# A trunk layer's mixer: sixth gate unit, first branch, softmaxes and convolution taps in another order on three engines

## The reference, cut to what matters

```python
o, s_f, s_b = _gla_bidir(qa, ka, va, glog[:, :, 0], glog[:, :, 1], s0[:, 0], s0[:, 1])
o = o * lax.rsqrt(jnp.mean(jnp.square(o), -1, keepdims=True) + LN_EPS) * lp['gla_norm']
y_a = (o.reshape(b_, l_, GLA_V_W) * jax.nn.silu(ra)) @ lp['w_br_gla']
...
y_b = att @ lp['w_br_na']        # neighbourhood attention; a softmax per head
y_c = _conv_module(cvi, lp)      # depthwise convolution of 31 taps, LayerNorm, silu, projection
g = jax.nn.sigmoid(mg.reshape(b_, l_, 3, D_MODEL))
m = g[:, :, 0] * y_a + g[:, :, 1] * y_b + g[:, :, 2] * y_c
return m @ lp['w_out'], kb, vb, jnp.stack([s_f, s_b], 1)
```

## Time and profile before

| | |
|---|---|
| median of 3 runs | 2106.37 us |
| the profiled execution | 2109.81 us, span 2107.6 us |
| PE busy | 1909.7 us (91% of the span) |
| DVE busy | 1461.7 us (69%) |
| ACT busy | 1135.2 us (54%) |
| mean granted TensorE clock | 0.954 of full |
| chain that ended last | PE 87%, DVE 6%, ACT 3%, issue 2%, DMA 1% |

### The profile page before, as it was taken

One profiled execution on the slowest core, in us unless ns is written; L12 is line 12 of the kernel. 1 busy time (PEld: TensorE's weight loads), 2 busy tenths in 40 slices (PEclk: granted clock), 3 DMA queues, 4 the chain that ended last, 5 costly groups with the idle time before them and its releaser, 6 DMA issues.

```text
span 2107.6 us, 25160 instructions
## 1 busy us (share of the span) xinstructions
PE 1909.7 (91%) x9102; PEld 1429.3 (68%) x9102; DVE 1461.7 (69%) x1795; ACT 1135.2 (54%) x1352; POOL 29.8 (1%) x53
## 2 busy tenths in 40 slices
PE   4999959869996999959789999999999999999994
PEld 1875435447884874434368888888888888888883
DVE  1446474344455445682489898998989899898995
ACT  2442220234442542221168777877878788787882
POOL 1000010000000000010000000000000000000000
PEclk8999979979998999979889999999999999999997
DMA  9565422445656455413269999999999999999990
GB/s 347 182 226 206 172 85 80 160 159 191 214 198 244 165 184 192 148 46 120 92 247 370 347 355 343 352 361 341 362 350 351 368 332 362 345 359 345 354 363 34
DMA packets 226992, 529.61 MB, mean 251 GB/s; under 512 B 4824, under 2 KB 7328, under 8 KB 226928
## 3 DMA queue, kind: packets, MB, share of 16 engines
q1 hardware_dynamic: 222848, 516.96, 68.0%
q0 software_dynamic: 3168, 9.80, 1.5%
q10 hardware_dynamic: 912, 1.97, 0.3%
HBM read 526.10 MB, written 2.62 MB: 251 GB/s over the span
## 4 chain that ended last, share of the span: by engine, by line
PE 87%; DVE 6%; ACT 3%; issue 2%; DMA 1%; ACTq 0%; DVEq 0%; POOL 0%; SPq 0%; POOLq 0%
PE ps L805 19%; PE ps L807 19%; PE ps L806 19%; PE ps L738 15%; PE ps L759 2%; PE ps L762 2%; PE ps L761 2%; PE ps L772 2%; PE ps L1139 2%; PE ps L795 1%; DVE arena L1821 1%; PE ps L1160 1%; DMA ring<-in_w_mod 1%; PE ps L1038 1%; ACT arena L1252 1%
## 5 line engine op out<-in xcount | busy, mean ns | idle before, releaser
L2092 DVE TENSOR_TENSOR arena_r<-ring,arena_r 128x1024 fp32r<-128x1024 f32 x448 | 540.0, 1223 | 38.3 <-ACT arena_r L1544 16.9
L1544 ACT ACTIVATE arena_r<-ring 128x1024 fp32r<-128x1024 f32 x448 | 474.1, 1061 | 119.0 <-PE ps L807 117.9
L805 PE MATMUL ps<-arena_r 128*128 128x512 f32 x1128 | 447.4, 397 | 22.2 <-DVE arena_r L1596 13.9
L806 PE MATMUL ps<-arena_r 128*128 128x512 f32 x1128 | 440.9, 391 | 0.0
L807 PE MATMUL ps<-arena_r 128*128 128x512 f32 x1128 | 411.8, 391 | 0.0
L2092 DVE TENSOR_TENSOR ring_r<-ring,ring_r 128x1024 fp32r<-128x1024 f32 x224 | 271.0, 1223 | 41.0 <-ACT ring_r L1544 38.0
L1544 ACT ACTIVATE ring_r<-ring 128x1024 fp32r<-128x1024 f32 x224 | 235.7, 1060 | 61.3 <-PE ps L807 60.3
L805 PEld LDWEIGHTS ps<-arena_r 128*128 128x128 f32 x1128 | 213.7, 189 | 67.7 <-issue 23.2
L805 PE MATMUL ps<-ring_r,arena_r 128*128 128x512 f32 (+1 forms) x592 | 239.3, 404 | 17.1 <-DVE ring_r L1596 8.3
L807 PEld LDWEIGHTS ps<-arena_r 128*128 128x128 f32 x1128 | 213.6, 189 | 46.5
L806 PEld LDWEIGHTS ps<-arena_r 128*128 128x128 f32 x1128 | 213.9, 190 | 43.9
(11 more groups left out here) (243 smaller groups left out, 1952.0 us busy)
## 6 DMA issues: line engine op xcount, KB each, us to landing
ring<-in_moe_w_gate SPq DMA_DIRECT2D x56, 2048.0 KB, 7.8
ring<-in_moe_w_up SPq DMA_DIRECT2D x56, 2048.0 KB, 8.0
ring<-in_moe_w_down SPq DMA_DIRECT2D x56, 2048.0 KB, 8.3
ring<-in_w_in SPq DMA_DIRECT2D x28, 2048.0 KB, 10.1
ring<-in_w_mod SPq DMA_DIRECT2D x24, 2048.0 KB, 8.6
ring<-in_ffd_w_gate SPq DMA_DIRECT2D x5, 2048.0 KB, 9.5
ring<-in_ffd_w_up SPq DMA_DIRECT2D x5, 2048.0 KB, 7.8
ring<-in_ffd_w_down SPq DMA_DIRECT2D x5, 2048.0 KB, 7.7
```

Source lines behind the costliest of these rows:

```text
L805: mm(o_, hi, w_hi[:, n], start=start, stop=False)
L806: mm(o_, hi, w_lo[:, n], start=False, stop=False)
L1544: act_(split_part(j)[0], raw_part(j), ACT.Copy).then_inc(part_hi, 1)
L2092: V.tensor_tensor(w_lo, raw_part(j), w_hi.bitcast(F32), ALU.subtract).then_inc(part_lo, 1)
```

## The change

Only the order of existing work changes; no arithmetic is added or left out. On PE, `gla_states(1)`, `kbtok`, the scores of group 0 and `gla_out(1)` now stand ahead of `mgate(5)`; `gla_turn(1)`, `kctxT` and the bias stand behind it; `cvtok` and `PT` of group 0 come next, then `branch(0)`; `cvT` and the scores of group 1 come behind `branch(0)`, then `branch(2)`; `gate_rows(0)` stands ahead of `branch(1)`. On DVE, ten taps stand between carry and norm of group 0, six inside `gla_prepare(1)` ahead of its wait for the exponentials, three behind it; `softmax(0)` follows `gla_norm(1)` at once; `diagonal` and `softmax(1)` stand between `gated(0)` and `gated(2)`. ACT follows: the first softmax's exponential stands ahead of the sixth gate unit. `plan()` lists products in the new order, so banks are handed out by it; the order of weight units stays.

```diff
@@ tensor @@
                 gla_scores(1)
-                mgate(5)
                 gla_states(1)
-                gla_out(1)
-                gla_turn(1)
                 turned(("kbtok", l), [kbT[:, j * T:j * T + P] for j in range(4)])
...
                     full(ins, "sc", l, 0, i)
+                gla_out(1)
+                mgate(5)
+                gla_turn(1)
+                pe.wait_ge(ctx_in, 16 * (l + 1))
+                turned(("kctxT", l), [kctx[:, j * P:(j + 1) * P] for j in range(4)])
...
+                copied("oT", l, 0), copied("oT", l, 1)
+                branch(0, lambda g, k: o[:, g * 512 + k * P:g * 512 + (k + 1) * P])
+                for g in range(G):
+                    copied("cvtok", l, g)
+                    turned(("cvT", l, g), [acc[:, g * 512 + j * P:g * 512 + (j + 1) * P] for j in range(4)])
                 copied("kctxT", l)
...
                 gate_rows(0, diag1)
+                copied("attT", l, 0), copied("attT", l, 1)
+                branch(1, lambda g, k: attT[:, g * 512 + k * P:g * 512 + (k + 1) * P])
                 mod_unit(l, 10, mrow)
@@ scalar @@
                 gla_keys(1)
+                take(kbtok, ("kbtok", l))
+                gla_sqrt()
+                softmax_exp(1024)
+                mgate(5)
+                gla_turned(1)
+                take(kctxT, ("kctxT", l))
+                for i in range(2):
+                    take(PT[:, i * 512:(i + 1) * 512], ("PT", l, 0, i))
+                norm_sqrt(2)
@@ vector @@
                     st.done(V.tensor_scalar(karg, karg, EXP_CAP, None, ALU.min), args_ready)
+                    if g:
+                        conv_taps(22, 28)
                     st.next(exps_ready)
...
                 gla_carry(0)
+                conv_taps(12, 22)
                 gla_norm(0)
                 gla_prepare(1)
-                conv_taps(12, 22)
+                conv_taps(28, TAPS)
                 gla_mask(1)
                 gla_carry(1)
                 gla_norm(1)
-                conv_taps(22, TAPS)
+                softmax(0)
                 mod_columns(4, 10, 32)
...
                 conv_norm()
-                softmax(0)
-                softmax(1)
...
                 gated(0)
+                diagonal(diag1, 16, 0)
+                softmax(1)
                 gated(2)
-                diagonal(diag1, 16, 0)
                 gated(1)
```

More of the change, by code:

```diff
@@ L167, in plan, with branch @@
         p("keT", l, 1), p("att", l, 1, 0), p("att", l, 1, 1)
+        p("kv", l, 1, 0), p("kv", l, 1, 1)
+        p("kbtok", l), p("sc", l, 0, 0), p("sc", l, 0, 1)
+        p("o", l, 1)
         mg(l, 5)
[L169 to L172, removed]
+        p("oT", l, 1)
+        p("kctxT", l), p("bias", l, 0), p("bias", l, 1)
         p("cvtok", l, 0), p("cvtok", l, 1)
-        p("cvT", l, 0), p("cvT", l, 1)
         p("PT", l, 0, 0), p("PT", l, 0, 1)
-        for i in range(4):
-            p("sc", l, 1, i)
-        for b in (0, 2):
+        def branch(b):
             for g in range(G):
@@ L181, in plan @@
             u(("br", l, b), ("y", l, b, 1, 1))
+        branch(0)
+        p("cvT", l, 0), p("cvT", l, 1)
+        for i in range(4):
+            p("sc", l, 1, i)
+        branch(2)
         p("attT", l, 0)
@@ L186, in plan @@
         for g in range(G):
-            p("y", l, 1, g, 0), p("y", l, 1, g, 1)
-        u(("br", l, 1), ("y", l, 1, 1, 1))
-        for g in range(G):
             p("gbc", l, 0, g, 0), p("gbc", l, 0, g, 1)
+        branch(1)
         mod(l, 10)
@@ L957, in _ @@
                 gla_scores(1)
-                mgate(5)
                 gla_states(1)
-                gla_out(1)
-                gla_turn(1)
                 turned(("kbtok", l), [kbT[:, j * T:j * T + P] for j in range(4)])
-                pe.wait_ge(ctx_in, 16 * (l + 1))
-                turned(("kctxT", l), [kctx[:, j * P:(j + 1) * P] for j in range(4)])
-                pe.wait_ge(bias_in, 64 * (l + 1))
-                for i in range(2):
-                    full(mm(claim("bias", l, i), C("flip"), bias[:, i * 512:(i + 1) * 512], start=True, stop=True),
-                         "bias", l, i)
                 for i in range(2):
@@ L976, in _ @@
                     full(ins, "sc", l, 0, i)
+                gla_out(1)
[3 more added lines that the diff above has]
+                turned(("kctxT", l), [kctx[:, j * P:(j + 1) * P] for j in range(4)])
+                pe.wait_ge(bias_in, 64 * (l + 1))
+                for i in range(2):
+                    full(mm(claim("bias", l, i), C("flip"), bias[:, i * 512:(i + 1) * 512], start=True, stop=True),
+                         "bias", l, i)
                 for g in range(G):
@@ L980, in _, with branch @@
                     turned(("cvtok", l, g), [acc[:, g * 512 + j * P:g * 512 + (j + 1) * P] for j in range(4)])
+                pe.wait_ge(P_ready, G * l + 1)
+                for i in range(2):
+                    turned(("PT", l, 0, i), [Pm[:, (4 * i + j) * P:(4 * i + j + 1) * P] for j in range(4)])
+                def branch(b, src):
+                    w = arrived(("br", l, b))
+                    for g in range(G):
+                        for n in range(2):
+                            tokens_times(("y", l, b, g, n), (lambda k, g=g: src(g, k)), w, ks=4, n0=512 * n)
+                copied("oT", l, 0), copied("oT", l, 1)
+                branch(0, lambda g, k: o[:, g * 512 + k * P:g * 512 + (k + 1) * P])
                 for g in range(G):
@@ L983, in _ @@
                     turned(("cvT", l, g), [acc[:, g * 512 + j * P:g * 512 + (j + 1) * P] for j in range(4)])
-                pe.wait_ge(P_ready, G * l + 1)
-                for i in range(2):
-                    turned(("PT", l, 0, i), [Pm[:, (4 * i + j) * P:(4 * i + j + 1) * P] for j in range(4)])
                 copied("kctxT", l)
@@ L996, in _ @@
                     full(ins, "sc", l, 1, i)
[L998 to L1005, removed]
                 copied("cvT", l, 0), copied("cvT", l, 1)
@@ L1028, in _ @@
                 na_values(1)
-                copied("attT", l, 0), copied("attT", l, 1)
-                branch(1, lambda g, k: attT[:, g * 512 + k * P:g * 512 + (k + 1) * P])
                 def gate_rows(j, d):
@@ L1408, in _ @@
                 mgate(4)
[L1409 to L1415, removed]
                 def softmax_exp(n):
@@ L1419, in softmax_exp @@
                     act_(Pm[:, 0:n], Pm[:, 0:n], ACT.Exp).then_inc(P_exp, 1)
+                gla_keys(1)
+                take(kbtok, ("kbtok", l))
[4 more added lines that the diff above has]
+                take(kctxT, ("kctxT", l))
+                for i in range(2):
+                    take(PT[:, i * 512:(i + 1) * 512], ("PT", l, 0, i))
+                norm_sqrt(2)
                 for g in range(G):
@@ L1428, in _ @@
                     free(ins, "cvT", l, g)
-                softmax_exp(1024)
-                for i in range(2):
-                    take(PT[:, i * 512:(i + 1) * 512], ("PT", l, 0, i))
                 softmax_exp(2048)
```

## The result

The changed kernel takes 2047.65 us (median of 4 runs, 2045.11 to 2053.18); the kernel before took 2106.24 us beside it on the same chip (4 runs, 2105.82 to 2109.25). The ratio is 0.9714, with an interval of 0.9701 to 0.9727. The forecast was 2047, and its range was 2040 to 2062.

A forecast was written before the change was run, and what follows sets the result against it. PE bounds the mixer, paying 22.4 us of waits on DVE, which idles 25.8 us under gate units. Savings of 30.0 and 29.2 us, together 59.1, from 2109.81 give 2050.7; less 3.4 to the median, 2047, range 2040 to 2062.

The forecast's parts named there:

- the tail: From the end of `branch(1)` to `mix`: merge, eight transpositions and ACT copies, 8.2 us, bounds 7.8 and 10.3.
- 0.3 for the keys: DVE inside `gla_prepare(1)`: 24 taps take 9.6 of 9.9 us left of the wait for ACT's exponentials, slack 0.3 us.
- 1.5 for the second softmax: `softmax(1)` on DVE: weights done at 316.5, PE asks at 317.0 + 1.05, slack 1.5 us.
- 4.7 of cover for the first: `softmax(0)` under the sixth gate unit: done at 279.3, PE asks at 284.0, leaving 4.7 us of cover.
- Table switches: ACT between `gla_sqrt` and the silu: six loads instead of three per layer not hidden, +7.7 us, 2055; chance 0.06.
- The second softmax: PE ahead of group 1's `PT`: `softmax(1)` ends last; 2054 if DVE is 5 us late, up to 2070; chance 0.08.
- The low clock: Moved PE work runs at 1.2 GHz, each branch 13.7 us longer; 2128 with all three branches; chance 0.02.
- That the change would not do what it says: A bank claim or a stream behind a wait ties PE to DVE's old pace; 2106; chance 0.04.
- the chain that ended last: Layer 0, sixth gate unit to first branch: chain leaves PE for 36 us, returning only with the branches at 320.03.
- The clock term at `mix`: Half-clock dip at the start of `mix`, which cost 1.7 us of work; taken as 0.
- goes (−1.7): Case in which the dip at the start of `mix` disappears, −1.7 us, beside staying (0) or doubling (+1.7).

The follow-up runs named there:

- order alone: Changed kernel with the convolution taps on DVE back where they stood before the change; 2104.41 us, ratio 0.9980.
- gate unit back: Changed kernel with the sixth gate unit back ahead of `gla_states(1)`, on PE, ACT and in the product list; 2068.78 us, ratio 0.9812.
- `cvT` back: Changed kernel with `cvT` turned ahead of `branch(0)` instead of behind it; 2067.28 us, ratio 0.9802.
- second softmax late: Changed kernel with `softmax(1)` on DVE behind `gated(2)` instead of ahead of it; 2084.61 us, ratio 0.9887.
- Taps alone: Kernel before the change with only the taps moved, PE and ACT in their old order; 2099.67 us, ratio 0.9950.
- the repeat: Changed kernel run once more, unaltered, on one chip beside a version with a shorter tail; 2049.01 us, ratio 0.9717.
- more table loads: Changed kernel with five unread small activations per layer on ACT that force ten more table loads in all; 2047.68 us, ratio 0.9713.

## Why the prediction was right

**The steps.** Counted from the end of the scores in layer 0, predicted against measured: the gate unit starts at 9.0 (8.9), `branch(0)` at 27.5 (27.1), `branch(2)` at 45.7 (45.3), `branch(1)` at 68.8 (68.5), the tail takes 8.2 (8.4), `mix` starts at 90.9 (90.8). The three slacks were near too: 0.3 for the keys (0.35), 1.5 for the second softmax (1.7), and 4.7 of cover for the first (about 5: done at 280.84, asked at 286).

**Why the sum held.** The waits that went are 22.4 us, and the second half is 30 shorter. The prediction did not subtract the waits: it set the new stream up row by row with durations from stretches at full clock, and checked that no wait would be left ahead of dense work. Four runs show what a subtraction misses, in layer 0, and in the last column for both layers what stands behind the second half:

| | second half grew | waits grew | slower rows behind them | `mix` above 27.70, layers 0 and 1 |
|---|---|---|---|---|
| order alone | 25.7 | 17.6 | 8.0 in four groups of rows | 3.0, 3.0 |
| gate unit back | 9.5 | 5.4 | 3.9 | 1.7, 1.7 |
| `cvT` back | 7.6 | 4.7 | 2.7 | 1.7, 1.7 |
| second softmax late | 15.6 | 13.9 | 1.7 | 3.0, 0.0 |

The growth of both second halves and of `mix` accounts for the times to about 1 us: for the order alone 51.6 + 6.0 = 57.6 against 56.8 measured, for the gate unit back 18.2 + 3.4 = 21.6 against 21.1, for `cvT` back 15.3 + 3.4 = 18.7 against 19.6, for the second softmax late 33.2 + 3.0 = 36.2 against 37.0. Where I did add up waits, in the expectations for the order alone and for `cvT` back, I fell short by the slower rows and by `mix`.

**What carries the gain.** Taps alone gain 7 to 8 us per layer, the order alone 3 to 4 us, both together 30 and 29. By themselves the two parts come to about two fifths of that: with the old order the taps free DVE while PE still has nothing dense to run during the norm and the softmax; with the old taps the output is 11.8 us late and everything behind it too. The prediction treated the two as one schedule and so did not have to divide it, but it also did not say that the parts lean on each other.

**The rivals.** Table switches: they cost nothing, shown by ten more of them. The second softmax: it ends in time by 1.7 us, and when it is moved the loss is 15.6 us. The low clock: it did not come, PE ran at 1.00 to the end of `branch(1)`; that it does come when a wait stands ahead is shown by the 0.50 of the run with the order alone, and by the slower rows of three others. That the change would not do what it says: no claim of a bank stops PE in its waits.

**What was off.** One row was misread: the chain that ended last comes back to PE at 312.77, with the turned weights of group 0, and not only with the branches at 320.03; it is away from PE for 34 us, and the scores ahead of the branches belong to it. The sum does not use this figure. The clock term at `mix` was taken as 0; against the 29.40 us of before it is −0.15 us in layer 0 and −1.7 in layer 1 of the profiled execution, and −1.7 in both layers of the repeat and of the run with more table loads, which have the same tail. So the choice "goes (−1.7)" was nearer than the 0. The stretches outside the second halves were taken as unchanged, and in the profiled execution they are 2.6 us longer in all, with what `mix` gave back already in them; among the kernels here they run from 253 to 260, 494 to 501 and 1111 to 1114 us, also between two executions of the same kernel (259.6 and 256.5). In the first stretch the runs show what differs: the changed kernel was granted a clock of 0.95 there in its first profiled execution, 0.97 in the repeat and 0.99 with more table loads; PE was busy for 220.6, 218.7 and 213.9 us and idle for 39.1, 37.9 and 39.5. So it is mostly the speed of PE's rows and less its waits; why the clock stayed low for longer in one execution than in another is left open. So the 2047 is right in its mechanism, and to within a few us it also had luck: the gain at `mix` that was left out and the longer stretches pull in opposite directions.

## What to carry to other kernels

Pair the waits: find where the helper engine idles under the main engine's dense work and where the main engine waits for the helper, and move both streams in one step, since half of the move may give nearly nothing. Cost a removed or added wait by writing the new stream forward in rows taken at full clock, with the half-clock work behind each wait counted, also in the next dense group behind the stretch. Then look at the last tail: once the middle is dense, the longest wait left is where the next few microseconds are.

## What the runs showed of the hardware

With `cvT` back, waits of 3.4 and 1.4 us on PE stood ahead of a branch that ran 1.55 us longer, while the waits of 0.7 and 0.9 us in the changed kernel left all three branches at 13.90; with the gate unit back, waits of 4.5 and 1.6 us left the branch at 13.90 too, and the small rows between took 8.7 us instead of 4.8. The tail has the same rows and the same waits of 0.7, 1.4 and 1.4 us in the changed kernel, in its repeat, with the gate unit back and with `cvT` back, and `mix` behind it took 29.25 and 27.70, twice 27.70, twice 29.40 and twice 29.40 us: the idle time right ahead of a dense group did not decide its clock by itself. A table load that belongs to an activation which has to wait for another engine runs ahead of that wait, and so costs nothing as long as the wait is longer: the load at 268.07 in the run with more table loads ends 1.30 us before its activation can start.
